# Reordering the VectorE work of the page chunks, the conv norm, the last V pages and the opening in a fused hybrid decoder step

## The reference

```
q, k, v, bg, u = mixer_inputs(rmsnorm(x), w_in)        # 6 x 512 columns; u = cg * xv
attn_prompt    = stick_breaking(q, k, v)               # causal, 8 heads of 64
attn_sample    = stick_breaking over the new tokens, then over 32 cache pages of 128 keys per sequence, newest first
c              = rmsnorm(bg * causal_conv3(u))
x = x + [rmsnorm(attn) | c] @ w_out
mk, mv = rmsnorm(mem) @ w_ck, rmsnorm(mem) @ w_cv      # 256 memory tokens
x = x + cross_attention(rmsnorm(x), mk, mv)            # the sample tokens read cached mk, mv
x = x + swiglu(rmsnorm(x));  y = rmsnorm(x)
```

## Time and profile before

| What | us |
|---|---|
| Median of three runs | 1208.37 |
| The three runs | 1208.37, 1198.38, 1223.24 |
| The profiled execution, whole time | 1211.09 |
| Its span (first to last instruction) | 1209.3 |
| TensorE busy | 1072.4 |
| VectorE busy | 665.9 |
| GpSimd busy | 409.9 |
| ScalarE busy | 321.4 |
| Mean granted TensorE clock | 0.948 of full |

### The profile page before, as it was taken

The page is one execution under the profiler, slowest core; times in us unless marked ns, Lnnn a source line. Parts: engine busy times, 40 slices in busy tenths (PEclk is TensorE's granted clock), DMA queues, the critical chain, the costliest instruction groups (busy, mean ns, idle before and its releaser), DMA issues.

```text
span 1209.3 us, 28991 instructions
## 1 busy us (share of the span) xinstructions
PE 1072.4 (89%) x11527; PEld 917.1 (76%) x11527; DVE 665.9 (55%) x909; ACT 321.4 (27%) x486; POOL 409.9 (34%) x341
## 2 busy tenths in 40 slices
PE   6889999996678867888599888899999999999997
PEld 3677887774445445556499858899999999999996
DVE  2745647677477676654379356755553002554544
ACT  3412121231233523333422153411211112112121
POOL 0524544442232233444332103343433333433330
PEclk9999999998888889889799999899999999999999
DMA  9888878779898787884652033223221233231222
GB/s 350 316 243 281 284 261 301 244 275 325 326 324 315 284 277 269 276 302 157 222 209 70 16 124 104 73 70 104 69 81 58 79 95 104 69 101 47 66 65 79
DMA packets 126501, 221.16 MB, mean 183 GB/s; under 512 B 9951, under 2 KB 68580, under 8 KB 126388
## 3 DMA queue, kind: packets, MB, share of 16 engines
q1 hardware_dynamic: 103234, 146.63, 36.5%
q0 software_dynamic: 20480, 67.13, 15.5%
q10 hardware_dynamic: 2674, 5.87, 1.3%
HBM read 213.78 MB, written 5.80 MB: 182 GB/s over the span
## 4 chain that ended last, share of the span: by engine, by line
PE 71%; DVE 11%; issue 6%; DMA 6%; SPq 3%; ACT 2%; POOL 1%; DVEq 0%; ACTq 0%; POOLq 0%
PE ps L519 37%; PE ps L1658 11%; PE ps L1761 9%; PE ps L1812 3%; DMA mw_raw<-in_w_in 2%; DMA k_set<-in_cache_sb_k 2%; PE ps L580 2%; DVE k_set L1335 2%; SPq L614 2%; DVE r_sq L693 1%; DVE r_sum L698 1%; SPq L615 1%; PE ps L363 1%; DVE h_lo L424 1%; PE ps L1715 1%
## 5 line engine op out<-in xcount | busy, mean ns | idle before, releaser
L475 POOL TENSOR_TENSOR w_lo<-w_raw,w_hi 128x2048 fp32r<-128x2048 f32 (+3 forms) x49 | 192.8, 3937 | 400.9 <-ACT w_hi L452 363.6
L1761 PE MATMUL ps<-k_set,q_blk 32*32 32x256 f32 x4096 | 142.0, 422 | 62.6 <-issue 47.6
L519 PE MATMUL ps<-h_hi,w_hi 128*128 128x288 f32 x832 | 180.5, 299 | 8.7 <-DVE h_lo L424 5.7
L519 PE MATMUL ps<-h_lo,w_hi 128*128 128x288 f32 x832 | 179.5, 298 | 0.0
L519 PE MATMUL ps<-h_hi,w_lo 128*128 128x288 f32 x832 | 179.4, 297 | 0.0
L1335 DVE STREAM_TRANSPOSE k_set<-k_set 128x1024 f32<-128x1024 f32 x128 | 150.1, 1219 | 37.4 <-DMA k_set<-in_cache_sb_k 36.1
L1761 PEld LDWEIGHTS ps<-k_set,q_blk 32*32 32x32 f32 x4096 | 82.5, 115 | 105.1 <-issue 68.7
L452 ACT ACTIVATE w_hi<-w_raw 128x2048 fp32r<-128x2048 f32 (+3 forms) x47 | 77.9, 1660 | 258.1 <-PE ps L519 228.5
L519 PEld LDWEIGHTS ps<-h_hi,w_hi 128*128 128x128 f32 x832 | 135.6, 191 | 9.8 <-issue 7.2
L964 POOL TENSOR_TENSOR mw_lo<-mw_raw,mw_hi 128x1024 fp32r<-128x1024 f32 x32 | 80.1, 2502 | 177.9 <-ACT mw_hi L1034 177.8
L615 POOL DMA_DIRECT2D v_late<-in_cache_sb_v x160 | 86.2, 539 | 159.4 <-issue 89.7
(11 more groups left out here) (263 smaller groups left out, 1698.9 us busy)
## 6 DMA issues: line engine op xcount, KB each, us to landing
k_set<-in_cache_sb_k SPq DMA_DIRECT2D x256, 256.0 KB, 4.7
v_late<-in_cache_sb_v POOLq DMA_DIRECT2D x160, 256.0 KB, 5.4
v_early<-in_cache_sb_v POOLq DMA_DIRECT2D x96, 256.0 KB, 5.4
mw_raw<-in_w_in SPq DMA_DIRECT2D x12, 1024.0 KB, 10.1
w_raw<-in_w_gate SPq DMA_DIRECT2D x11, 1024.0 KB, 5.4
w_raw<-in_w_up SPq DMA_DIRECT2D x11, 1024.0 KB, 5.3
w_raw<-in_w_down SPq DMA_DIRECT2D x8, 768.0 KB, 4.3
w_raw<-in_w_down SPq DMA_DIRECT2D x8, 640.0 KB, 4.0
```

What stands on the lines that cost most here:

```text
L475: return nc.gpsimd.tensor_tensor(w_lo[s][:, ks, :], w_raw[s][:, ks, :], w_hi[s][:, ks, :].bitcast(F32), ALU.subtract)
L519: op = nc.tensor.matmul(ps[:, 2 * t + hf, 0:b - a], weights[s][:, k, t * P:(t + 1) * P], x[:, k0 + k, a:b], start=begin and k == ks[0] and ...
L1761: op = nc.tensor.matmul(tiled(ps[c:c + 32, a, 0:2 * P], 32), blk[r, n:n + 32], k_set[s][r, :, d:d + 32], start=e == 0 and j == 0, stop=e = ...
```

## The change

1. **Page chunks, VectorE's order.** Now: add_sums(C - 1), sample rows, prompt weights, queries, K blocks 0 and 1, the memory tile's evacuation, K blocks 2 and 3, the low parts of the memory operand (chunk 20), page weights, new weights.
2. **Conv norm.** It moves from chunk 11, after add_sums(10), to the end of chunk 10, ahead of the K blocks of half 13.
3. **The last eight V pages** (248 to 255, chunk 31) go into k_set[1] instead of the ring, with two semaphores of their own, and wait for the scores of half 31 instead of a summed page.
4. **The opening.** tile(2) is computed between memory_rms and half_scores(1, 0), its evacuation comes after new_weights(0), ScalarE copies the new weights and makes the high part of tile 3 ahead of page_sigmoids(0), new_weight_transposes(0) moves between the two halves of half_scores(1), and all K blocks of half 0 come ahead of the evacuation of tile 1. Chunk 0 has no tile(2), and its tile(3) comes behind weight_transposes(0) and ahead of half_scores(2).

```
@@ -265,6 +265,7 @@
                                               "rows", "rows_tr", "rows_copied")}
         s_kp = [[sem(f"k_pages{s}_{i}") for i in range(2)] for s in range(2)]
         s_v = [sem(f"v_pages{i}") for i in range(RING // 2)]
+        s_v_last = [sem(f"v_last_pages{i}") for i in range(2)]
         s_kt, s_vsum = sem("k_blocks_transposed"), sem("v_page_summed")
         c_ = {n: sem(f"cross_{n}") for n in ("score", "max", "exp", "prob", "tr", "tr_copied", "out", "out_copied",
                                              "queries", "zeroed", "rows", "rows_tr")}
@@ -340,6 +341,9 @@
         MEM_TILES = {C: TILES + i for i, C in enumerate((22, 23, 25, 26, 27, 28, 29, 30))}
 
         def v_place(n):
+            if n >= 8 * (CHUNKS - 1):
+                m = n - 8 * (CHUNKS - 1)
+                return k_set[1][:, m:m + 1, :], s_v_last[m // 4], 64
             place = n % RING
             return (v_late if n >= 8 * LAST else v_early)[place][:, :, :], s_v[place // 2], 32 * (n // RING + 1)
 
@@ -641,7 +645,9 @@
         def v_pages(pool, pages):
 
             for n in pages:
-                if n >= RING:
+                if n >= 8 * (CHUNKS - 1):
+                    pool.wait_ge(m_["half"], CHUNKS)
+                elif n >= RING:
                     pool.wait_ge(s_vsum, n - RING + 1)
                 if n == 8:
                     pool.wait_ge(s_sq["ck"], 2)
@@ -1127,7 +1133,7 @@
             def group(g, last):
                 for c in range(8):
                     C, u = 8 * g + c, 8 * g + c - LAST
-                    if 2 * C + 3 < TILES:
+                    if C and 2 * C + 3 < TILES:
                         tile_hi(2 * C + 3)
                     if 3 <= u < 19:
                         prompt_out(u - 3)
@@ -1200,8 +1206,9 @@
             new_sigmoids(0)
             act.wait_ge(s_ms["ck"], 1)
             nc.scalar.activation(rstd_m[:, :], ps[:, 6, 0:NMEM], ACT.Copy).then_inc(s_rt["ck"], 1)
+            copy_new_weights(0)
+            tile_hi(3)
             page_sigmoids(0)
-            copy_new_weights(0)
             for g in range(GROUPS):
                 group(g, g == GROUPS - 1)
 
@@ -1429,7 +1436,8 @@
                 k_blocks(C + 2, range(4))
                 if c == 0 and g:
                     sample_rows(g)
-                evac(2 * C + 2)
+                if C:
+                    evac(2 * C + 2)
                 if C in (2, 4):
                     convolve(C // 2 - 1)
                 if C in (3, 5):
@@ -1446,6 +1454,7 @@
                 if c == 6:
                     new_weights(g + 1)
                 if C == LAST - 2:
+                    conv_norm()
                     k_blocks(C + 3, range(4))
 
             def page_chunk(g, c):
@@ -1455,29 +1464,26 @@
                 if C == LAST - 1:
                     evac(TILES - 1)
                 add_sums(C - 1)
-                if C == LAST - 1:
-                    conv_norm()
-                if more and C >= LAST:
-                    k_blocks(C + 3, range(2))
                 if c == 0:
                     sample_rows(g)
                 if 1 <= u < 17:
                     prompt_weights(u - 1)
                 if c == 5 and g < GROUPS - 1:
                     queries(g + 1)
+                if more:
+                    k_blocks(C + 3, range(2))
                 if C in MEM_TILES:
                     evac(MEM_TILES[C])
+                if more:
+                    k_blocks(C + 3, range(2, 4))
                 if C == 20:
                     lo_parts(dve, "ck", mT, G_MEM, range(KD))
                 if c % 2 and C + 1 < CHUNKS:
                     page_weights(C // 2 + 1)
                 if C == LAST - 1:
                     step(dve, nc.vector.memset(q_blk[1][:, :], 0.0))
-                    k_blocks(C + 3, range(2))
                 if c == 6 and g < GROUPS - 1:
                     new_weights(g + 1)
-                if more:
-                    k_blocks(C + 3, range(2, 4))
 
             def add_sums(C):
 
@@ -1525,9 +1531,8 @@
             dve.wait_ge(s_rt["inb"], 1)
             evac(0)
             queries(0)
-            k_blocks(0, range(2))
+            k_blocks(0, range(4))
             evac(1)
-            k_blocks(0, range(2, 4))
             dve.wait_ge(s_sq["ck"], 3)
             step(dve, nc.vector.reciprocal(x_ss[:, 5:7], x_ss[:, 5:7]))
             for m in range(MT):
@@ -1535,6 +1540,7 @@
             op.then_inc(s_sum["ck"], 1)
             k_blocks(1, range(4))
             new_weights(0)
+            evac(2)
             page_weights(0)
             for g in range(GROUPS):
                 group(g, g == GROUPS - 1)
@@ -1831,18 +1837,22 @@
                     rms_pe(pe, "conv", c_sq[:, 0, :], T, None, 0)
                 if c == 0 and g:
                     new_weight_transposes(g)
-                tile(2 * C + 2)
+                if C:
+                    tile(2 * C + 2)
                 if c == 0 and g:
                     sample_rows(g)
                 weight_transposes(C)
                 if C == 10:
                     pe.wait_ge(s_rt["conv"], 1)
+                if C == 0:
+                    tile(3)
                 half_scores(C + 2, 0)
                 half_scores(C + 2, 1)
                 if c == 0 and g:
                     new_sums(g)
                 sums(C, (0, 1))
-                tile(2 * C + 3)
+                if C:
+                    tile(2 * C + 3)
                 if c == 6:
                     new_scores(g + 1)
                 sums(C, (2, 3))
@@ -1908,9 +1918,10 @@
             half_scores(0, 0)
             half_scores(0, 1)
             memory_rms()
+            tile(2)
             half_scores(1, 0)
+            new_weight_transposes(0)
             half_scores(1, 1)
-            new_weight_transposes(0)
             pe.wait_ge(s_rt["ck"], 1)
             new_sums(0)
             for C in range(CHUNKS):
```

## The result

Over 20 runs each the changed kernel takes 1193.3 us and the kernel before 1211.3; the ratio is 0.9869, 95% interval 0.9844 to 0.9894. That is 1.3% faster (16 us by the ratio; the two medians lie 18 apart), where 1172 (3.2%) had been forecast. The profiled execution of the change has a span of 1195.0 us, 14.3 less than before.

The account below looks back on a forecast made before the run. TensorE's work was taken as the bound, so only its waits can be won. From 1211.1 us: -18 (447 to 570) -23 (280 to 447) +1 (norm) -4 (V pages) +6 (opening) = -38, forecast 1172, range 1152 to 1198.

Parts of the forecast that it names:

- K blocks ahead of page weights: Even page-chunk borders: TensorE's wait for scores goes; a border had cost 5.5 us plus 1.7 of halved clock.
- issue wait under 2 us: Sign at even chunk borders 14 to 28: TensorE's issue wait under 2 us, first 64 scores at 1.96 us.
- Stage 447 to 570 us: Later page chunks: 25.3 us of waits and clock, less 4.2 and 3 of new waits, 18 us won (8 to 25).
- three new waits of 1.4: Stage 447 to 570 us: add_sums, now behind the page weights, makes TensorE wait 1.4 us three times, 4.2 in all.
- Rival D: Page weights, behind the last K page, come late if pages take 18 us: 447 to 570 gives 4, total 1186; 0.25 with A.
- Stage 280 to 447 us: Earlier page chunks: 59 us of waits and clock, but DMA at 366 GB/s allows 23 us won (10 to 31).
- rival A: DMA takes back half, K pages landing later: 12 us won in each page stage, 4 at the end, total 1190; 0.25 with D.
- The opening: Chunk 0 onward: slot 3, behind half 4 on SP, issued about 93.8, tile(6) at 112.9; 6 us lost.
- Conv norm: Chunk 10: the moved norm delays K blocks of half 13, so TensorE begins chunk 11 later; 1 us lost.
- Last V pages: Chunk 31: eight pages there by 580, before the sums, no wait; w_out's low part next; 4 us won (3 to 7).
- Rival B: Weight slots land late in odd tile chunks 3 to 9 too, 33 us lost, total 1222; chance 0.07.
- C: Rival: opening costs nothing, first page stage gives 31, second 25, end 7; 63 us won, total 1148; chance 0.13.

Follow-up runs that it names:

- e10: e9 with the page weights moved from the end of odd page chunks to right behind add_sums in the following even chunk: 1177.5 us, 0.9743 of the kernel before.
- e16: The change with the page weights behind add_sums of the even page chunks: 1187.8 us, 0.9792 of the kernel before.
- e9: e3 with the last eight V pages put in the free K set and issued by SP: 1181.4 us, 0.9758 of the kernel before.
- e8: e3 with the memory tile's evacuation ahead of all four K blocks: 1183.9 us, 0.9794 of the kernel before.
- e7: e3 with only the first 256 of 512 columns of V pages 108 to 255 loaded (result not the reference's): 1167.6 us, 0.9649 of the kernel before.
- e1: The change with its opening undone, the other parts kept: 1184.0 us, 0.9802 of the kernel before.
- e3: The kernel before with VectorE's new order in the page chunks and conv norm in chunk 10 alone: 1184.3 us, 0.9807 of the kernel before.
- e5: The change with K blocks 0 and 1 put back ahead of sample rows, prompt weights and queries: 1192.1 us, 0.9877 of the kernel before.
- e12: e2 with SP issuing weight slot 3 ahead of the K pages of half 4: 1207.0 us, 0.9968 of the kernel before.
- e2: The kernel before with the new opening alone: 1215.8 us, 1.0047 of the kernel before.

## Why the prediction was off, step by step

**K blocks ahead of page weights: right in kind.** The borders of halves 20, 22, 26 and 28 lost their wait and those of 14 and 24 kept 0.1 and 1.3 us. But its sign "issue wait under 2 us" failed at half 16 (10.0 us), half 18 (3.3) and half 30 (3.8). What it priced too high was the net.

**Stage 447 to 570 us: the step that failed.** Of 18 us and the 4 for the V pages, 8.3 came by the end of the sums and 6.4 by the start of w_out. The sum was 25.3 - 4.2 - 3. Its first term held four waits for K blocks, 18.5 us, and those were there before. The step that failed is what it left standing: three waits of 1.4 and 3 us at chunk 28, 7.2 in all. In the change there are 4.5 and 3.8 ahead of scores, 2.1, 2.1 and 1.6 for o_sum and 2.8 for the evacuation: 17.0 in all. So 1.5 us of these waits were won instead of 11.3; another 2.9 at the V pages of chunk 31 (7.1 to 4.2). The clock was forecast at 6.8, 4 x 1.7, and TensorE's busy time fell by 4.8: one of the four borders had no halved clock to win back, since the 64 matmuls behind its wait took 1.96 us before too.

```profile
464.59 1.96 PE L1761 MATMUL ps<-k_set,q_blk 32*32 32x256 f32 x64 [2.50 <-DVE k_set L1335]
```

The waits term by term:
- "three new waits of 1.4" were 2.1, 2.1 and 1.6. The working set the page weights' scan 0.9 us before TensorE is free; K blocks 2 and 3 now stand ahead of it, and it starts 0.2 to 1.1 us before. In e10 and e16, where these waits are gone, the stage is 8.3 and 4.9 us shorter in one trace each; the totals of e9 and e10 can't be told apart.
- The evacuation behind K blocks 0 and 1, 2.8 us, was not in the sum. In e8 that wait went without a gain that shows.
- The wait for half 27, 4.5 us, was put at nothing: the sum took a load to last the 13.5 us of the opening's rows. From the release of the set to the last landing no half from 14 on kept to that in the change (14.4 us at best), nor in the kernel before (13.6 to 26.6); half 27 took from 460.7 to 480.3 and half 30 from 506.1 to 524.9, 19.6 and 18.8. The sentence "the DMA doesn't forbid it" went by the bytes of the whole stage (share 0.76), where the window rows of the change show 1.03 and 1.01 in just the stretches of these two loads. Rival D had named this mechanism, with pages that take 18 us, and priced it for all borders; in this stage it came at two.

With the o_sum waits and the V pages out of the way (e10), stage 2 gives 148.4 - 127.0 = 21.4 us, of which 4.7 are lost again ahead of w_out: 16.7 of the forecast 22, though K pages are still waited for. So most of the gain could be had, and VectorE's new order hid a part of it. How the rest divides between the order and the traffic is not shown: e7 has lighter pages and the old o_sum waits, e10 the reverse, and no run has both removed.

**Stage 280 to 447 us: right in kind, somewhat high.** Forecast 23 of 59, since the DMA forbids more. Measured 17.0 in the change, 18.8 in e1 and 21.6 in e3. The share rose to 0.95, as it said, but the rate only to 335 GB/s, where the 23 rests on 366 and rival A had 340. e7 shows the DMA as part of the bound: 24.7 us with lighter pages, still far from 59, so it is not the whole of it.

The 17 us are not spread evenly. Up to half 16 only 3 were won, behind it 14. The waits of 9.9 for half 14 and 6.8 for the queries went, and 4.8 for half 15 and 10.0 for half 16 stand in the place of 2.7, in a stretch in which the DMA engines are full (share 1.04 from 305 to 330 us). In every version with the new order and full pages this wait is 9.1 to 17.0 us, but for e5, where the queries' wait takes its place; with lighter pages (e7) it is 4.4. The K pages land later by what TensorE is earlier: here rival A is right.

**The opening: right.** Slot 3 was issued at 97.05 (forecast 93.8), tile(6) at 115.95 (112.9), half_scores(2) ended at 88.1 (84.7); 5.7 to 8 us lost (6). Of the 3.4 us more, 1.3 lie ahead of the weight transposes (75.1 instead of 73.8, behind the 5.5 us wait; 1.1 of them are there already at tile 2's low part, which GpSimd begins at 55.92 and not at 54.86), 0.5 in them and 1.7 in tile(3), both at half clock (8.33 us instead of 6.6). e12 shows SP's queue as the cause, as argued.

**Conv norm: right.** The scores of half 13 waited 1.03 us for K blocks (1 us).

**Last V pages: wrong, small.** Forecast 4, and no wait left; e1 against e3 shows none in the total. In the change the wait fell by 2.9 us, and 1.9 were lost again between the sums and w_out. "They are there by 580" took GpSimd to be free at 566. It had a low part and pages 244 to 247 ahead of them, so issues ran from 560.96 to 569.04, although the scores of half 31 were done at 553.0. Even in time (e9) they win little: w_out's weights and c_lo come next.

In sum: opening and norm 8.9 lost instead of 7, stage 1 17 instead of 23, stage 2 and the end 6.4 (8.3 less the 1.9 at w_out) instead of 22. The price of rival A, 1190, was near, but partly by luck: it had 12 and 12 us for the stages and 4 for the end, and 17.0, 8.3 and a loss of 1.9 came; in the second stage as much was lost to VectorE's order (8.7 us of waits) as to K pages (8.3). Rival B did not come: between tile(6) and half 12 the only wait for an evacuation is one of 1.1 us, which stood there before too. Neither did C.

Left open: why e3 and e9, the same up to the last chunk, differ by 3.4 us in stage 1; and what would bring half 16 sooner, which starts at 327 to 330 in versions with the new order and full pages whose half 12 starts at 267 to 272. The traces put it on the transfers there (full share, 27 to 32 us from release to landing, 23 and a start at 325.1 in e7), but no run took traffic from that stretch alone.

## What to carry to other kernels

When a stall is removed by putting work behind it, price everything that is queued after the moved instruction against what TensorE wants next; here, in the second stage, the waits that came nearly equalled those that went, and moving one more block (the page weights, behind the short add) shortened that stage by 5 to 8 us in the traces, which the totals bear out only in part. A mean DMA share of 0.77 says nothing of a single load: look at the window of the load that must be in time, and take its duration from that stage, not from a quieter one. In the issuing queue here, one weight slot with an early need did better ahead of eight pages that wait for a later event (e12 against e2).

## What the hardware showed that was not expected

The DMA engines moved more than the 386 GB/s of the earlier trace rows. The window of e3:

```profile
305.00:330.00 25.00, 10.97 (x229) 6.30 (x237) 12.42 (x36) 4.07 (x7) 7.58 (x15) 0.72 1.04 404
```

404 GB/s over 25 us at full share, where other full windows of the change gave 364 and 363: the rate at which the share reads full varies by 11%. The Trainium skill, "DMA: Bandwidth & Descriptors", section "Bandwidth", puts the HBM side at about 358 GB/s per core, and its note on its own measurements gives it as what each core gets when both cores that share the memory are streaming. The windows here, of a program on one core, lie above it, so it was no bound in them.
